# x tiles in the SSD stage's places, and bf16 weight copies made in device memory, in an eight-core gMLP and SSD block kernel

## What is computed

```python
h = rms_norm(x, norm_w)
proj = h @ w_in                       # u, v, z_a | z_b, xBC, dt | gate logits
y_a = gmlp_spatial_gating(u, v, z_a, ln_v_w, ln_v_b, w_spatial, b_spatial)
y_b = ssd_branch(z_b, xbc, dt_raw, conv_w, conv_b, dt_bias, a_log, d_skip, ssm_norm_w)
branch_d = einsum('bsne,ned->bsnd', stack([y_a, y_b]), w_branch)
gates = sigmoid(gate_logits + b_gate)
merged = sum(gates * branch_d)        # over the two branches
x = x + merged @ w_out
out = rms_norm(x, final_norm_w)
```

## Time and profile before

| | |
|---|---|
| median of three runs | 3256.91 us |
| the profiled execution's own time | 3255.04 us |
| its span on the slowest core (5) | 3253.5 us |
| spans of the eight cores | 3246.1 to 3253.5 us |
| PE busy | 3045.9 us, 94% of the span |
| DVE / ACT / POOL busy | 51% / 40% / 14% |
| weight loads | 808 of 512 KB (bf16 side), 9.6 us median to landing |
| HBM read / written | 911.66 MB / 16.78 MB |

### The profile page before, as it was taken

One profiled execution on the slowest core, in us unless ns is written; L12 is line 12 of the kernel. 1 busy time (PEld: TensorE's weight loads), 2 busy tenths in 40 slices (PEclk: granted clock), 3 DMA queues, 4 the chain that ended last, 5 costly groups with the idle time before them and its releaser, 6 DMA issues.

```text
span 3253.5 us, 50395 instructions; the slowest of 8 cores (3246.1 to 3253.5 us)
## 1 busy us (share of the span) xinstructions
PE 3045.9 (94%) x16134; PEld 1446.1 (44%) x16134; DVE 1655.3 (51%) x2618; ACT 1292.0 (40%) x2716; POOL 440.4 (14%) x831
## 2 busy tenths in 40 slices
PE   6999989999999879999999789999999699999997
PEld 2444444444444334444444344444444344444443
DVE  3888875676422256666212466665222566663114
ACT  4677646555311035555211145553111255552111
POOL 2111111111111101111111111111111011111110
PEclk9999999999999989999999899999999899999998
DMA  9988987898899978887999888778999888878996
GB/s 209 176 156 159 181 146 118 133 145 132 142 179 184 187 163 143 134 138 131 163 190 172 183 167 135 132 131 139 180 187 181 186 134 133 136 132 147 152 154 159
DMA packets 161103, 507.97 MB, mean 156 GB/s; under 512 B 18000, under 2 KB 18256, under 8 KB 160848
## 3 DMA queue, kind: packets, MB, share of 16 engines
q0 software_dynamic: 116496, 423.81, 79.0%
q1 hardware_dynamic: 44352, 80.94, 9.1%
HBM read 911.66 MB, written 16.78 MB: 285 GB/s over the span
## 4 chain that ended last, share of the span: by engine, by line
PE 61%; DVE 17%; DMA 8%; issue 7%; ACT 6%; DVEq 1%; SPq 0%; ACTq 0%
PE ps L631 49%; DVE sb_cacc L1147 6%; PE ps L650 4%; DMA sb_xt<-x_all 4%; PE ps L634 3%; DMA out<-sb_yac 2%; DMA sb_ybuf<-x_all 1%; ACT sb_dec L959 1%; DVE sb_xdec L1177 1%; DVE sb_scT L1239 1%; ACT sb_dec L974 1%; DVE sb_ybuf L1270 1%; ACT sb_cacc L877 1%; DVE sb_hT L1038 1%; DVE sb_yac L1253 1%
## 5 line engine op out<-in xcount | busy, mean ns | idle before, releaser
L631 PE MATMUL ps<-sb_hT,sb_ring 128*128 128x512 bf16 x7440 | 1704.3, 381 | 17.6 <-DVE sb_cbs L1221 8.4
L631 PEld LDWEIGHTS ps<-sb_hT,sb_ring 128*128 128x128 bf16 x7440 | 723.9, 98 | 873.1 <-issue 46.6
L552 POOL DMA_DIRECT2D sb_ring<-wn x808 | 429.3, 533 | 2762.1 <-PE ps L634 2408.1
L1147 DVE SCALAR_TENSOR_TENSOR sb_cacc<-sb_xpre,sb_cols,sb_cacc 128x512 f32<-128x512 f32 x672 | 502.8, 750 | 294.7 <-ACT sb_cacc L877 245.5
L631 PE MATMUL ps<-sb_ybuf,sb_ring 128*128 128x512 bf16 x1920 | 435.3, 379 | 0.7 <-DVE sb_ybuf L1270 0.7
L1124 DVE TENSOR_TENSOR sb_dec<-sb_dec,ps 128x512 f32<-128x512 f32 x128 | 88.1, 688 | 640.1 <-PE ps L634 639.9
L631 PE MATMUL ps<-sb_vm,sb_ring 128*128 128x512 bf16 x1680 | 387.3, 384 | 7.2 <-DVE sb_vm L1130 7.2
L894 ACT ACTIVATE sb_dec<-ps,sb_cols 128x512 f32<-128x512 f32 x128 | 88.0, 688 | 677.5 <-PE ps L634 677.4
L631 PEld LDWEIGHTS ps<-sb_ybuf,sb_ring 128*128 128x128 bf16 x1920 | 187.5, 98 | 228.2 <-issue 2.5
L631 PEld LDWEIGHTS ps<-sb_vm,sb_ring 128*128 128x128 bf16 x1680 | 164.4, 99 | 204.5 <-issue 18.2
L650 PE MATMUL ps<-sb_ring,sb_hT 128*128 128x512 bf16 x1024 | 236.8, 385 | 10.8 <-DVE sb_cbs L1221 5.5
(11 more groups left out here) (167 smaller groups left out, 2512.0 us busy)
## 6 DMA issues: line engine op xcount, KB each, us to landing
sb_ring<-wn POOLq DMA_DIRECT2D x808, 512.0 KB, 9.6
sb_xt<-x_all SPq DMA_DIRECT2D x112, 256.0 KB, 9.3
sb_ybuf<-x_all SPq DMA_DIRECT2D x80, 256.0 KB, 17.9
out<-sb_e SPq DMA_DIRECT2D x32, 256.0 KB, 2.2
out<-sb_yac SPq DMA_DIRECT2D x32, 256.0 KB, 2.2
sb_cacc<-x_all SPq DMA_DIRECT2D x30, 256.0 KB, 13.9
sb_xpre<-x_all SPq DMA_DIRECT2D x18, 256.0 KB, 18.9
sb_dec<-wst SPq DMA_DIRECT2D x1, 512.0 KB, 14.0
```

The lines of the kernel that those rows point to most:

```text
L552: e.dma_start(out=ring[:, i % NSLOT, :], in_=wn[block_of(name, n)]).then_inc(*on("w%d" % (i % NSLOT), WEIGHTS[i], by=16))
L631: e.matmul(pb(b), lhsT=wv[:, kc, :], rhs=rhs[kc], start=(kc == 0), stop=False)
L1147: e.scalar_tensor_tensor(out=cacc[:, m % NCA, :], in0=xpre[:, m % NCV, t:t + 512], scalar=cols[:, C_CW + 32 * t + ci:C_CW + 32 * t + ci + ...
```

## The change

It has three parts.

1. **x tiles.** The 16 `sc` tiles of the next pass get a place each (`homes`): the seven of before, and nine in SSD tiles that lie idle in the merge stage (`xTg`, `szb`, `scT`, `BTg`, `CTg`, `xdec`). They are loaded once, in the merge stage, two behind each `g0` block, and serve the squares too, whose units are now 2.1 beats apart from beat 101 (before 3.0 from 100). The residual tiles get a ring of eight (`xt`, `gz`, `gmx`, `cbs`, half of `e2`): the first eight are loaded in the merge stage, the others each when the tile eight before has been added.
2. **Copies.** 80 blocks (`o` 16, `b1`, `g1`, `b0`, `g0` 16 each) are copied once from `wn` (f32) to a new tensor `wb` (bf16) in device memory, by casting DMAs on POOL's queue: 28 in pass 4, 28 in pass 5, 24 in pass 6, every 3 beats from beat 2 to beat 83 of the SSD stage. A copy waits for the one four before it.
3. **Loads.** From the pass in which a block was copied, its load reads `wb` (bf16 to bf16, 512 KB) in place of `wn`.

```diff
@@ plan_main
-        plan_norm(pl, p + 1, b + 100.0, 3.0, b + 160.6, 0.62)
+        plan_norm(pl, p + 1, b + 101.0, 2.1, b + 160.6, 0.62)
@@ make_schedule
-        if u[0] == "sc" and u[1] > 4:
-            early = u[2] < NXS
-            pl.put(pass_start(u[1] - 1) + 120.0 + 3 * u[2] if early else next(t for t, _, v in pl.items if v == ("sc", u[1], u[2] - NXS)) + 0.25, "xs", u[1], u[2])
-        if (u[0] == "sq" and u[1] > 4) or (u[0] == "ev" and u[2] == "o"):
-            uses.append((beat, u))
-    for i in range(NXT, len(uses)):
-        pl.put(uses[i - NXT][0] + 0.25, "xr", i)
+        if u[0] == "sq" and u[1] > 4:
+            pl.put(pass_start(u[1] - 1) + 98.2 + 2 * u[2], "xs", u[1], u[2])
+        if u[0] == "ev" and u[2] == "o":
+            b, d = pass_start(u[1]), u[3]
+            pl.put(b + 130.0 + 4 * d if d < NRS else b + 161.5 + d - NRS, "xr", u[1], d)
...
+COPIED = [("o", d) for d in range(16)] + [(n, d) for n in ("b1", "g1", "b0", "g0") for d in range(15, -1, -1)]
+COPY_PASS = {w: 4 + k // 28 for k, w in enumerate(COPIED)}
+COPY_AT = {w: k for k, w in enumerate(COPIED)}
+NCP = 4
+def from_copy(w):
+    return w[1:] in COPY_PASS and w[0] >= COPY_PASS[w[1:]]
...
+STREAM = [(BEAT[weight_given_back(WEIGHTS[i - NSLOT])], 0, i) for i in range(NSLOT, len(WEIGHTS))]
+STREAM += [(pass_start(COPY_PASS[w]) + 2.0 + 3.0 * (k % 28), 1, k) for w, k in COPY_AT.items()]
...
+        homes = [cacc[:, i, :] for i in range(NCA)] + [xpre[:, i, 0:512] for i in range(NCV)]
+        for pair in (xTg[:, 0], xTg[:, 1], szb[:, 0], szb[:, 1], scT[:, 0:2], scT[:, 2:4], BTg[:], CTg[:]):
+            homes.append(pair.rearrange("p j t -> p (j t)").bitcast(F32))
+        homes.append(xdec[:].rearrange("p c n -> p (c n)").bitcast(F32))
+        residual = [xt[:, i, :] for i in range(NXT)] + [gz[:, 0, :], gz[:, 1, :], gmx[:], cbs[:], e2[:, 1, :]]
@@ sync
                     if k == 0:
                         e.wait_ge(*at("si", p - 1, "C", 7))
-                        e.wait_ge(*at("ho", p - 1, "C", 7))
-                    if k >= NXS:
-                        e.wait_ge(*at("hT", p, k - NXS))
...
+                        e.wait_ge(*at("Hn", p - 1, 7, 3))
+                        e.wait_ge(*at("yg", p - 1, 7))
+                    if k % 2 == 0:
+                        e.wait_ge(*at("pj", p - 1, "g0", k // 2))
+                    e.dma_start(out=homes[k], in_=x_all[p][:, k * 512:(k + 1) * 512]).then_inc(*on("xl%d" % k, p, by=16))
                 elif u[0] == "xr":
-                    i = u[1]
-                    e.wait_ge(*at(*x_given_back(XUSE[i - NXT])))
-                    load_ring(i)
+                    _, p, d = u
+                    if d == 0:
+                        e.wait_ge(*at("ga", p, 15))
+                    if d < NRS:
+                        e.wait_ge(*at("pj", p, "g0", 8 + d))
+                    else:
+                        e.wait_ge(*at("xn", p, d - NRS))
+                    e.dma_start(out=residual[d % NRS], in_=x_all[p][:, d * 512:(d + 1) * 512]).then_inc(
+                        *on("xr%d" % (d % NRS), p, d, by=16))
@@ gpsimd, load(i)
-                e.dma_start(out=ring[:, i % NSLOT, :], in_=wn[block_of(name, n)]).then_inc(
+                w = WEIGHTS[i]
+                if from_copy(w):
+                    e.wait_ge(*at("cp%d" % (COPY_AT[w[1:]] % NCP), w[1:]))
+                e.dma_start(out=ring[:, i % NSLOT, :], in_=(wb if from_copy(w) else wn)[block_of(name, n)]).then_inc(
@@ gpsimd
-            for i in range(NSLOT, len(WEIGHTS)):
-                load(i)
+            for is_copy, i in STREAM:
+                if is_copy:
+                    w = COPIED[i]
+                    if i >= NCP:
+                        e.wait_ge(*at("cp%d" % (i % NCP), COPIED[i - NCP]))
+                    e.dma_start(out=wb[block_of(*w)], in_=wn[block_of(*w)]).then_inc(*on("cp%d" % (i % NCP), w, by=16))
+                else:
+                    load(i)
@@ vector, the residual add
-                        x_here(e, u)
+                        e.wait_ge(*at("xr%d" % (i % NRS), p, i))
-                        e.tensor_tensor(out=xnew[:, i, :], in0=xtile(u), in1=pb(b), op=ALU.add).then_inc(*on("xn", p, i))
+                        e.tensor_tensor(out=xnew[:, i, :], in0=residual[i % NRS], in1=pb(b), op=ALU.add).then_inc(*on("xn", p, i))
```

More of the change, by code:

```diff
@@ L21 @@
 NXT = 3
+NRS = 8
 NCV = 3
 NCA = 4
-NXS = NCV + NCA
 C_NW, C_LNW, C_LNB, C_CW, C_CB, C_SNW, C_BG, C_FW, C_DS, C_FLAG = 0, 16, 32, 48, 176, 208, 224, 256, 272, 288
@@ L224, in make_schedule @@
         plan_main(pl, p)
-    uses = []
     for beat, _, u in sorted(pl.items):
@@ L230, in make_schedule @@
             pl.put(beat + 0.3, "xl", u[1] + 1, u[2])
-        if u[0] == "sc" and u[1] > 4:
-            early = u[2] < NXS
-            pl.put(pass_start(u[1] - 1) + 120.0 + 3 * u[2] if early else next(t for t, _, v in pl.items if v == ("sc", u[1], u[2] - NXS)) + 0.25, "xs", u[1], u[2])
-        if (u[0] == "sq" and u[1] > 4) or (u[0] == "ev" and u[2] == "o"):
-            uses.append((beat, u))
-    for i in range(NXT, len(uses)):
-        pl.put(uses[i - NXT][0] + 0.25, "xr", i)
-    return pl.order(), {u: beat for beat, _, u in pl.items}, [u for _, u in uses]
-SCHED, BEAT, XUSE = make_schedule()
-X_AT = {u: i for i, u in enumerate(XUSE)}
+        if u[0] == "sq" and u[1] > 4:
[3 more added lines that the diff above has]
+            pl.put(b + 130.0 + 4 * d if d < NRS else b + 161.5 + d - NRS, "xr", u[1], d)
+    return pl.order(), {u: beat for beat, _, u in pl.items}
+SCHED, BEAT = make_schedule()
 CONVS = [u[1:] for u in SCHED if u[0] == "ev" and u[2] in ("x", "B", "C")]
@@ L263, in weight_given_back @@
     return ("ch", p, i) if name == "C" and not is_main(p) else ("pj", p, name, i)
-def x_given_back(u):
-    return ("sqp",) + u[1:] if u[0] == "sq" else ("xn", u[1], u[3])
 def bank_given_back(u):
@@ L333 @@
 BANK, BANK_FREE = bank_plan()
+STREAM = [(BEAT[weight_given_back(WEIGHTS[i - NSLOT])], 0, i) for i in range(NSLOT, len(WEIGHTS))]
+STREAM += [(pass_start(COPY_PASS[w]) + 2.0 + 3.0 * (k % 28), 1, k) for w, k in COPY_AT.items()]
+STREAM = [u[1:] for u in sorted(STREAM)]
 class Signals:
@@ L369, in _build @@
     wn = nc.dram_tensor("wn", [NBLK, 128, 2048], F32, kind="ExternalInput").ap()
+    wb = nc.dram_tensor("wb", [NBLK, 128, 2048], BF16, kind="Internal").ap()
     wdt_d = nc.dram_tensor("wdt", [128, 512], F32, kind="ExternalInput").ap()
@@ L478, in xtile @@
         def xtile(u):
[L480 to L493, removed]
+            return homes[u[2]] if u[1] > 4 else xnew[:, u[2], :]
         def back2(p, g):
@@ L503, in sync @@
         def sync(e):
[L504 to L508, removed]
             for k in range(16):
@@ L516, in sync @@
             e.dma_start(out=dec[:, 0:2, :].rearrange("p a t -> p (a t)"), in_=bsb_d[:, :]).then_inc(*on("kbs", by=16))
-            for i in range(NXT):
-                load_ring(i)
             for u in SCHED:
@@ L528, in sync @@
                         e.wait_ge(*at("si", p - 1, "C", 7))
-                        e.wait_ge(*at("ho", p - 1, "C", 7))
-                    if k >= NXS:
-                        e.wait_ge(*at("hT", p, k - NXS))
-                    e.dma_start(out=xtile(("sc", p, k)), in_=x_all[p][:, k * 512:(k + 1) * 512]).then_inc(
-                        *on("xl%d" % (k % NXS), p, k, by=16))
-                elif u[0] == "xr":
-                    i = u[1]
-                    e.wait_ge(*at(*x_given_back(XUSE[i - NXT])))
-                    load_ring(i)
+                        e.wait_ge(*at("Hn", p - 1, 7, 3))
[3 more added lines that the diff above has]
+                    e.dma_start(out=homes[k], in_=x_all[p][:, k * 512:(k + 1) * 512]).then_inc(*on("xl%d" % k, p, by=16))
+                elif u[0] == "xr":
+                    _, p, d = u
[7 more added lines that the diff above has]
+                        *on("xr%d" % (d % NRS), p, d, by=16))
                 elif u[0] == "fo":
@@ L797, in scalar @@
                     _, p, kc = u
-                    x_here(e, u)
+                    e.wait_ge(*at("xl%d" % u[2], u[1]))
                     if p > 4:
```

## The result

The changed kernel takes 3341.64 us (median of four runs), the one before 3258.35 us beside it: a ratio of 1.0256, 95% interval 1.0233 to 1.028. It is slower by 83 us; the forecast was 3238 us. In some runs the cores of one die take longer at a lower granted clock, and all ratios here leave such runs out.

The account below looks back on a forecast made before the run. TensorE, busy 94% of the span, bounds the kernel, with DMA engines the other near-bound. 3255 - 63 (x tiles) + 40 (copies in the SSD stages) + 6 (pass starts) = 3238 us; range 3192 to 3298.

Parts of the forecast that it names:

- What bounds the kernel, and the gain of the x tiles: TensorE busy 94%; earlier x tiles remove the out-stage stall of passes 4 to 6 before `da`, gaining 63 us.
- The copied weights in merge and out: Halved weight loads gain nothing: TensorE is already full in merge, and the out stage's stall was not a weight's.
- The copies in the SSD stages: In passes 4 to 6, copies beyond the free DMA time make TensorE wait: losses 21 + 19 + 0 = 40 us.
- The cost, c = 4.2: DMA time of one copy in the SSD stages, taken as 4.2 us, between bounds of 3.2 and 4.8.
- The room, 97, 99 and 110 us: DMA time copies can take in the SSD stages of passes 4, 5 and 6 before TensorE waits.
- The ring's lead: Weight ring in each SSD stage may run down from 8 blocks to 1, adding 7 x 3.2 = 22 us.
- The clock: Lower clock behind each starved SSD-stage block might add 10 to 20 us; not in the forecast sum.
- rival 2: Copies starve TensorE in the SSD stages of passes 4 to 6; 3250 to 3322 us, chance 0.27.
- The pass starts, 6 us: Copies delay the final norm's stores at the starts of passes 5 and 6: 3 us each, bounds 0 and 8.
- rival 3: Copies block stores and loads behind them, or take over 5.4 us each: loss 130 us or more, over 3322, chance 0.09.
- Rival 1: Copies nearly free in the SSD stages, up to 3.6 us each: 3198 to 3206 us, chance 0.27.
- rival 4: The x part leaves the out-stage stall, as something else holds hT: 3295 us or more, chance 0.05.

## Why the prediction was wrong

**What bounds the kernel, and the gain of the x tiles: right.** 63 us were forecast. The out stages won 65, the wait of 60.0 us is gone, `da` follows its block at once, the clock is 1.00, and the x part alone moved the time by 65 us. But the same stall would have gone by the cheaper `o` loads. The forecast took "the out stage's stall was not a weight's" as reason to give the copied weights nothing; in the copies-only run the old x loads come in time as soon as the weights beside them are halved. In the sum this hid nothing, as the stall can be removed only once.

**The copied weights in merge and out: right in the sum.** Merge stays at 222 us, and a copied block costs about what was assumed: 0.50 x 222 / 64 = 1.7 us of all engines in pass 7's merge stage. The 19 us between used and unused copies exist only because the copies fill the queues.

**The copies in the SSD stages: the step that failed.** 40 us were forecast, 154 measured (13 of them at the pass starts, below). The sum had two terms, the cost of a copy and the room for it. Both were too kind; the room carries most of the error.

- *The cost, c = 4.2*: too low, but inside its bounds of 3.2 and 4.8. By share times length, pass 4's stage held 1.01 x 427 = 431 us of DMA work, for 0.81 x 380 = 308 before: 123 us for 28 copies, 4.4 each. Passes 5 and 6 give the same: (446 - 324) / 28 and (424 - 319) / 24 = 4.4. This is net of work put off: in the DMA records 468 and 458 fewer weight rows than before (4096 bytes each, 128 a block) start inside the stages of passes 4 and 5, about 3.6 blocks or 12 us in each. Gross, the records give for pass 4 4.03 us for an engine's 64 KB row in the mean, and 431 ns for 403 for each of 11659 weight rows, which is 0.7 us a copy more: 4.7, and likewise 4.8 and 4.5 in passes 5 and 6. So the reading that a copy costs more than a load, since it writes device memory as well, fits. The 4.9 us that I had estimated from the Trainium skill's page DMA: Bandwidth & Descriptors (Latency and other measured facts) lie a little above this, and much nearer than the load's 3.2.
- *The room, 97, 99 and 110 us*: wrong. At the gross costs the losses of 47, 60 and 47 us leave rooms of about 85, 75 and 60 us. The trace shows where the difference went.
  - The ring's lead was counted as 22 us a pass. It gave 12 in passes 4 and 5 and nothing in pass 6: at the start of `g0` two blocks had landed and were not yet used up, the one just starting included, where it was six before; in pass 6 it was six again. And it was spent well before the stage's end: from beat 61 to beat 80, in all three passes, only the block just starting had landed.
  - The cheap loads for merge were counted as 3, 6 and 13 us. In pass 4 there are none: its first eight merge blocks all come from `wn`, since the `b1` blocks of the first columns are copied in pass 5.
  - The free share was taken as a mean over the stage, but it can be used only where a copy lies. Copies came every 3 beats; the load beside them was uneven.

Beats 0 to 16 and 16 to 32 of pass 4, before, then after:

```profile
472.00:535.00 63.00, 63.00 (x390) 30.95 (x389) 34.43 (x60) 35.28 (x77) 8.96 (x15) 0.97 0.60 96
535.00:599.00 64.00, 63.35 (x352) 31.15 (x350) 41.68 (x67) 32.80 (x73) 7.40 (x14) 1.00 0.89 145
```

```profile
470.00:533.00 63.00, 63.00 (x392) 30.98 (x391) 34.87 (x60) 35.25 (x77) 11.54 (x20) 0.98 0.85 122
533.00:613.00 80.00, 67.00 (x349) 32.29 (x348) 41.15 (x66) 33.22 (x74) 9.97 (x19) 0.91 1.02 148
```

The first stretch had room to spare and left 0.15 of its DMA time unused; the second had 7 us free, was given five or six copies of 4 us or more, and grew by 16 us. After, beats 0 to 16, 16 to 32 of pass 5 and beats 80 to 96 of pass 6:

```profile
1184.00:1270.00 86.00, 64.67 (x300) 28.97 (x299) 42.07 (x66) 31.64 (x71) 11.03 (x21) 0.86 0.82 147
1270.00:1349.00 79.00, 67.14 (x346) 32.12 (x345) 41.75 (x67) 32.66 (x71) 9.97 (x19) 0.91 1.02 150
2300.00:2362.00 62.00, 61.96 (x353) 30.67 (x351) 38.78 (x56) 22.41 (x45) 7.92 (x15) 1.00 0.90 178
```

At the start of passes 5 and 6 (0.82 in pass 6 too, over 85 us) TensorE and DVE stood for each other and for stores, and some 15 us of the DMA engines' time went unused; behind the last copy of pass 6 another 6. Free share plus ring, less this unused time, is 72 + 12 = 84, 71 + 12 - 15 = 68 and 75 - 15 - 6 = 54 us, where 85, 75 and 60 were found; the few us left may be the cheap loads, of which passes 5 and 6 have 4 and 8. This is an account of where time went unused, not an experiment: no run places the copies by the free share of each stretch.

- *The two together*: with the forecast rooms the losses would have been 28 x 4.4 - 97, 28 x 4.4 - 99 and nothing, 50 us, at the net cost, and about 70 at the gross costs. So 10 to 30 us of the error of 114 are the cost's, and 84 to 104 the room's.

**The clock: a term put at nothing in the sum.** TensorE's own time in these three stages of core 5 adds up to nearly the same loss: 97.7 us of waits for weight blocks, 13 of longer waits for the C tile, and 41 us in which it was busy longer with the same number of matmuls and transposes, at a granted clock of 0.94 to 0.96 for 0.98 to 0.99. The prediction named this only under rival 2, with 10 to 20 us.

**The pass starts, 6 us: mis-sized.** TensorE's wait for the C tile grew from 8.1 to 15.1 us in pass 5 and from 8.8 to 15.0 in pass 6, 13 us in all; 7 a pass is inside the bounds of 0 and 8, above the 3 taken. That moving the norm units wins 17 us even without copies, the forecast had not asked: it had read these waits as a fixed part of the kernel.

**The rivals.** Rival 2 was the right mechanism in the right place, starved blocks in the SSD stages, and so was its clock remark. It was given 0.27 and an end at 3322, since its losses were worked out with the same rooms. The time, 3342 us, and the loss, 154 us, lie where the prediction had put rival 3 (130 us or more, over 3322, chance 0.09), but for neither of its reasons: short rows cost the same, and c stayed under 5.4. Rival 1 is refuted: its 3198 to 3206 needed copies at a loss of at most 8 us. So is rival 4, as the stall went. The range, which ended at 3298 although rival 2 alone was said to reach 3322, missed by 44 us because every case in it shared one term, the room, that had been given no bounds at all.

## What to carry to other kernels

Work moved into another stage's free DMA share is paid in full once the share is used up. Count the room stretch by stretch, where the work will lie, and not as a mean over the stage; count of the prefetch ring's lead at most what the next stage can pay back (12 of 22 us here, in two of three passes); and give the room bounds as well as the cost. Before cheaper loads are bought with extra traffic, ask whether the stage that they serve waits for loads at all; here merge was bound by TensorE, and the out stage's one stall went for nothing by asking for 24 tiles earlier. Two edits that cure the same stall don't add; run each alone.

## What the runs showed of the hardware

- A casting copy from device memory to device memory, 1 MB read and 0.5 MB written, held each of the 16 DMA engines for 4.03 us (one 64 KB row an engine; pass 4's mean, weight blocks beside it 8 x 0.431 = 3.4 us), and for 3.5 us in the same pass with half as many copies. The same copy as eight rows of 8 KB an engine changed the kernel's time by no more than 10 us in 3342.
- In pass 4's SSD stage a mean DMA share of 0.96 cost nothing (381 us with 28 stores of 512 KB), one of 0.97 to 0.99 cost 4 to 14 us, and at 1.01 the stage's length followed the work. The mean alone does not tell: pass 6's stage of the changed kernel lost 47 us at a mean of 0.96, made of stretches at 0.82 and at 1.02.
- With the copies in the queues the weight rows of the same core took longer, 431 ns for 403 in pass 4 (425 with half as many copies); which side of the copies does it is open.
- At the start of pass 5, stores of 256 KB landed in 6.1 us in the median and 28.6 us at most with copies in the queues; in the kernel before it was 2.5 and 16.1 us.
